# The opening of a two-layer backbone step, gone through input block by input block

## What is computed

```python
D_MODEL, D_FF, SEQ, DEC_SEQ = 1024, 2816, 128, 512
def _mods(cvec, w_ada, b_ada):
    m = jax.nn.silu(cvec) @ w_ada + b_ada
    return m.reshape(cvec.shape[0], 1, N_MOD, D_MODEL)
def _modulate(x, mods, i):
    return x * (1.0 + mods[:, :, 3 * i + 1]) + mods[:, :, 3 * i]
def _swiglu(u, w_up, w_down):
    a, g = jnp.split(u @ w_up, 2, axis=-1)
    return (jax.nn.silu(g) * a) @ w_down
def _ffn_sublayer(x, mods, i, w_up, w_down, ln_g, ln_b):
    y = _swiglu(_modulate(x, mods, i), w_up, w_down)
    return _post_norm(x, y, mods, i, 0.5, ln_g, ln_b)
```

## Time and profile before

| | us |
|---|---|
| median of 3 runs (2974.46 to 2975.7) | 2975.05 |
| the profiled execution, device time | 2975.69 |
| its span, first to last instruction | 2973.9 |
| TensorE matmuls busy in it | 2777.2 (93%) |
| DVE busy | 1711.2 (58%) |
| ACT busy | 766.6 (26%) |

### The profile page before, as it was taken

The page is one execution under the profiler, slowest core; times in us unless marked ns, Lnnn a source line. Parts: engine busy times, 40 slices in busy tenths (PEclk is TensorE's granted clock), DMA queues, the critical chain, the costliest instruction groups (busy, mean ns, idle before and its releaser), DMA issues.

```text
span 2973.9 us, 47454 instructions
## 1 busy us (share of the span) xinstructions
PE 2777.2 (93%) x18760; PEld 2733.3 (92%) x18760; DVE 1711.2 (58%) x3152; ACT 766.6 (26%) x1091; POOL 0.2 (0%) x4
## 2 busy tenths in 40 slices
PE   0599999989999999999999999998999999999994
PEld 0599999989899999999999999998989999999994
DVE  4465555754566685454576555575456668444456
ACT  0211211343322251121252121134332225111124
POOL 0000000000000000000000000000000000000000
PEclk9899999999999999999999999999999999999997
DMA  6233233212133223223313323322213322322320
GB/s 224 79 128 111 102 130 118 79 68 77 54 128 114 99 86 113 99 99 105 117 61 128 113 99 134 114 78 68 77 53 128 114 98 86 113 99 100 112 85 36
DMA packets 76870, 299.34 MB, mean 101 GB/s; under 512 B 24769, under 2 KB 29121, under 8 KB 52673
## 3 DMA queue, kind: packets, MB, share of 16 engines
q1 hardware_dynamic: 50496, 214.31, 20.8%
q10 hardware_dynamic: 26240, 83.20, 8.3%
HBM read 293.80 MB, written 6.82 MB: 101 GB/s over the span
## 4 chain that ended last, share of the span: by engine, by line
PE 89%; DVE 5%; SPq 4%; issue 2%; ACT 1%; DMA 0%; DVEq 0%; ACTq 0%
PE psum L527 11%; PE psum L526 11%; PE psum L524 11%; PE psum L384 6%; PE psum L385 6%; PE psum L382 6%; PE psum L427 3%; PE psum L430 3%; PE psum L431 3%; SPq L299 3%; PE psum L744 3%; PE psum L747 3%; PE psum L746 3%; PE psum L468 2%; PE psum L472 2%
## 5 line engine op out<-in xcount | busy, mean ns | idle before, releaser
L524 PE MATMUL psum<-Uh,w_hi 128*128 128x320 f32 x2304 | 711.9, 309 | 0.0
L526 PE MATMUL psum<-Ul,w_hi 128*128 128x320 f32 x2304 | 711.9, 309 | 0.0
L527 PE MATMUL psum<-Uh,w_lo 128*128 128x320 f32 x2304 | 711.9, 309 | 0.0
L810 ACT ACTIVATE w_hi<-w_raw 128x2048 fp32r<-128x2048 f32 x170 | 325.1, 1912 | 611.4 <-PE psum L382 318.9
L1101 DVE TENSOR_TENSOR w_lo<-w_raw,w_hi 128x2048 fp32r<-128x2048 f32 x170 | 389.5, 2291 | 82.0 <-ACT w_hi L810 76.8
L526 PEld LDWEIGHTS psum<-Ul,w_hi 128*128 128x128 f32 x2304 | 432.5, 188 | 0.0
L527 PEld LDWEIGHTS psum<-Uh,w_lo 128*128 128x128 f32 x2304 | 432.5, 188 | 0.0
L524 PEld LDWEIGHTS psum<-Uh,w_hi 128*128 128x128 f32 x2304 | 432.5, 188 | 0.0
L1284 DVE TENSOR_TENSOR hf<-sg,psum 128x320 f32<-128x320 f32 x176 | 85.7, 487 | 423.6 <-ACT sg L898 421.7
L385 PE MATMUL psum<-Hh,w_lo 128*128 128x320 f32 x1024 | 316.2, 309 | 0.0
L382 PE MATMUL psum<-Hh,w_hi 128*128 128x320 f32 x1024 | 316.2, 309 | 0.0
(11 more groups left out here) (223 smaller groups left out, 5183.7 us busy)
## 6 DMA issues: line engine op xcount, KB each, us to landing
w_raw<-in_wstream SPq DMA_DIRECT2D x188, 1024.0 KB, 4.9
ada_w<-in_ada ACTq DMA_DIRECT2D x145, 512.0 KB, 3.6
ada<-in_ada SPq DMA_DIRECT2D x4, 2048.0 KB, 19.9
gath<-in_rpb SPq DMA_DIRECT2D x128, 24.0 KB, 2.2
G<-gath ACTq DMA_DIRECT2D x4, 768.0 KB, 4.5
X<-in_xT SPq DMA_DIRECT2D x8, 320.0 KB, 14.2
yT<-X SPq DMA_DIRECT2D x8, 320.0 KB, 3.4
mask<-in_mask ACTq DMA_DIRECT2D x2, 384.0 KB, 5.0
```

The source lines that it names most:

```text
L524: m1 = pe.matmul(out, wh, rh, start=(k == 0), stop=False)
L526: pe.matmul(out, wh, rl, start=False, stop=False)
L527: mm = pe.matmul(out, wl, rh, start=False, stop=(k == KD - 1))
L810: act.activation(hi, w_raw[:, r, :, :], ACT.Copy).then_inc(s_whi, 1)
```

## The change

The opening is written as one function on each engine (`opening`), used for the first sub-layer of layer 0; `first_up` stays for the others.
- SyncE loads block by block: two chunks (shift and scale of block k) and x's block k, each a load of its own, into twelve places (`first_w`) used in turn. Blocks 0 and 1 come first, then weight tiles 0 and 1, then blocks 2 to 5, a wait for the first eight sums, blocks 6 and 7, and then the constants. Weight tiles 2 to 19 are loaded by a written-out loop; from tile 4 on, eight gathers follow each load.
- ACT loads `c`, `bada`, `c_ctx`, in this order, with a Silu of one column ahead. It makes u for a block as soon as this block's sums are there, and also the rounded `Uh`, which DVE did before.
- DVE does the sums of blocks 0 and 1 for both vectors; then, for half 0, those of `c` alone for blocks 2 to 7, with the low part `Ul` of the block before in between; and those of `c_ctx` for blocks 2 to 7 in half 1. `bada` (and `bada` + 1, kept in `lnm`) is the sum's starting value. The constants' copies and the scaling of `X` come at the end.
- TensorE goes over the blocks for tiles 0 and 1, from block 4 on with tile 2 too (blocks 0 to 3 of it made up at once), then half 1 of the three, then tile 3 for both halves. At the end it waits for `s_init` 4 and `s_cst`.
- `craw`, `cst` are at other places; the first chunk for the later sums (`load_ada(FIRST_ADA, 0)`) is asked for after tile 3 is rounded.

The declarations are left out here, and the functions `first_up` without `pending`.

```diff
+        def first_mods_ready(v, k):
+
+            if k < 2:
+                return 4 * k + 2 * v + 2
+            return 8 + 2 * (k - 1) + 2 * (KD - 2) * v
...
         @block.sync
         def _(sp):
-            for q in range(4):
-                n = FIRST_ADA // 4
-                sp.dma_start(ada0[:, q * n:(q + 1) * n, :],
-                             a["ada"][q * n:(q + 1) * n].rearrange("c p k -> p c k")).then_inc(s_ada0[q], 16)
-            for k in range(KD):
-                sp.dma_start(X[:, k, :], a["xT"][k]).then_inc(s_x, 16)
-            sp.dma_start(cst[:, :, :], a["dft_small"]).then_inc(s_cst, 16)
+            def first_block(k):
+                for j in range(2):
+                    sp.dma_start(first_w[(2 * k + j) % 12], a["ada"][j * KD + k]).then_inc(s_ada0[k], 16)
+                sp.dma_start(X[:, k, :], a["xT"][k]).then_inc(s_x[k], 16)
+
+            for k in range(2):
+                first_block(k)
+            for s in range(2):
+                sp.dma_start(w_raw[:, s, :, :], a["wstream"][s]).then_inc(s_wload[s], 16)
+            for k in range(2, 6):
+                first_block(k)
+            sp.wait_ge(s_first, first_mods_ready(1, 1))
+            first_block(6)
+            first_block(7)
             sp.dma_start(ident[:, :], a["eye"]).then_inc(s_cst, 16)
             sp.dma_start(lng[:, :], a["lng"]).then_inc(s_cst, 16)
             sp.dma_start(lnb[:, :], a["lnb"]).then_inc(s_cst, 16)
-            for s in range(2):
-                sp.dma_start(w_raw[:, s, :, :], a["wstream"][s]).then_inc(s_wload[s], 16)
-
-            for c in range(QTILE):
-                for r in range(ROWS):
-                    src = a["rpb"][:, ROWS - 1 - r:2 * ROWS - 1 - r, QTILE - 1 - c:QTILE - 1 - c + TW]
-                    sp.dma_start(a["gath"][:, c * ROWS + r, :, :], src).then_inc(s_gath, 16)
-
-            with sp.Fori(1, DEPTH * TILES // 2) as j:
+            sp.dma_start(cst[:, :, :], a["dft_small"]).then_inc(s_cst, 16)
+
+            for t in range(2, 20):
+                sp.wait_ge(s_wsplit, t - 1)
+                sp.dma_start(w_raw[:, t % 2, :, :], a["wstream"][t]).then_inc(s_wload[t % 2], 16)
+                if t >= 4:
+                    c = t - 4
+                    for r in range(ROWS):
+                        src = a["rpb"][:, ROWS - 1 - r:2 * ROWS - 1 - r, QTILE - 1 - c:QTILE - 1 - c + TW]
+                        sp.dma_start(a["gath"][:, c * ROWS + r, :, :], src).then_inc(s_gath, 16)
+
+            with sp.Fori(10, DEPTH * TILES // 2) as j:
...
+            def opening():
+
+
+                def block_products(t, u, h, k):
+                    for b in range(2):
+                        wh, wl = [w[:, b * KD + k, :] for w in t]
+                        rh, rl = half(Uh, Ul, h)(k)
+                        out = bank(u, b, 0, HT)
+                        m1 = pe.matmul(out, wh, rh, start=(k == 0), stop=False)
+                        if (t, h, b, k) == (tiles[0], 0, 0, 0):
+                            started(m1)
+                        pe.matmul(out, wh, rl, start=False, stop=False)
+                        mm = pe.matmul(out, wl, rh, start=False, stop=(k == KD - 1))
+                    if k == KD - 1:
+                        filled(mm)
+
+                tiles = [take(), take()]
+                us = [next_use(), next_use()]
+                for k in range(KD):
+                    if k == 4:
+                        tiles.append(take(spare_f))
+                        us.append(next_use())
+                        for j in range(4):
+                            block_products(tiles[2], us[2], 0, j)
+                    u_ready(0, k)
+                    for t, u in zip(tiles, us):
+                        block_products(t, u, 0, k)
+                us = [next_use() for _ in tiles]
+                for k in range(KD):
+                    u_ready(1, k)
+                    for t, u in zip(tiles, us):
+                        block_products(t, u, 1, k)
+                late = take(spare_h)
+                one(late, 0, 2)
+                one(late, 1, 1)
+                C["u"].next(2 * KD)
+                pe.wait_ge(s_init, 4)
+                pe.wait_ge(s_cst, 64)
...
-            pe.wait_ge(s_init, 3)
-            pe.wait_ge(s_cst, 64)
...
+            def opening():
+
+                def first_input(h, k):
+                    i = h * KD + k
+                    act.wait_ge(s_first, first_mods_ready(h, k))
+                    if h == 0:
+                        act.wait_ge(s_x[k], 16)
+                    if i >= 4:
+                        act.wait_ge(s_u, i - 3)
+                    for lo, hi, v in SEGS[h]:
+                        q = act.activation(u32[:, k % 4, lo - h * HT:hi - h * HT], X[:, k, lo:hi],
+                                           ACT.Identity, bias=mods[0][:, v, k:k + 1],
+                                           scale=mods[0][:, v, KD + k:KD + k + 1])
+                    q.then_inc(s_u32, 1)
+                    act.wait_ge(s_u32, i + 1)
+                    act.activation(Uh[:, k, h * HT:(h + 1) * HT], u32[:, k % 4, :], ACT.Copy).then_inc(s_fu, 1)
+
+                for v in range(2):
+                    act.dma_start(craw[:, v, :], a["c" if v == 0 else "c_ctx"].partition_broadcast(P))\
+                        .then_inc(s_craw[v], 16)
+                    if v == 0:
+                        act.dma_start(bada[:, :], a["bada"]).then_inc(s_bada, 16)
+                act.wait_ge(s_init, 1)
+                act.activation(warm[:, :], epsc[:, :], ACT.Silu)
+                for v in range(2):
+                    act.wait_ge(s_craw[v], 16)
+                    act.activation(csilu[:, v, :], craw[:, v, :], ACT.Silu).then_inc(s_csilu, 1)
+                first_input(0, 0)
+                round_tile()
+                first_input(0, 1)
+                round_tile(1)
+                first_input(0, 2)
+                first_input(0, 3)
+                act.wait_ge(s_csilu, 2)
+                round_tile(2, spare_f)
+                for k in range(4, KD):
+                    first_input(0, k)
+                for k in range(3):
+                    first_input(1, k)
+                gate_half()
+                gate_half()
+                for k in range(3, 6):
+                    first_input(1, k)
+                gate_half()
+                for k in range(6, KD):
+                    first_input(1, k)
+                act.wait_ge(s_first, first_mods_ready(1, KD - 1))
+                round_tile(2, spare_h)
+                load_ada(FIRST_ADA, 0)
+                for _ in range(3):
+                    gate_half()
+                round_tile(1)
+                ada_pair()
+                gate_half()
+                gate_half()
+                ada_pair()
...
+            def opening(chunks):
+
+                taken = [0]
+
+                def first_mod(v, k):
+                    for j in range(2):
+                        if taken[0]:
+                            dve.wait_ge(s_first, taken[0])
+                        start_at = (bada[:, k:k + 1], lnm[:, 0, 0, k:k + 1])[j]
+                        dve.tensor_tensor_reduce(junk[:, :], first_w[(2 * k + j) % 12], csilu[:, v, :], 1.0, start_at,
+                                                 ALU.mult, ALU.add, mods[0][:, v, j * KD + k:j * KD + k + 1])\
+                            .then_inc(s_first, 1)
+                        taken[0] += 1
+
+                def first_low(h, k):
+                    cols = slice(h * HT, (h + 1) * HT)
+                    dve.wait_ge(s_fu, h * KD + k + 1)
+                    dve.tensor_tensor(Ul[:, k, cols], u32[:, k % 4, :], Uh[:, k, cols].bitcast(F32), ALU.subtract)\
+                        .then_inc(s_u, 1)
+
+                dve.wait_ge(s_bada, 16)
+                dve.tensor_scalar(lnm[:, 0, 0, :], bada[:, KD:2 * KD], 1.0, None, ALU.add).then_inc(s_init, 1)
+                dve.wait_ge(s_init, 2)
+                for k in range(2):
+                    dve.wait_ge(s_ada0[k], 32)
+                    for v in range(2):
+                        dve.wait_ge(s_csilu, v + 1)
+                        first_mod(v, k)
+                low_tile()
+                low_tile()
+                for k in range(KD):
+                    if k >= 2:
+                        dve.wait_ge(s_ada0[k], 32)
+                        first_mod(0, k)
+                    if k >= 1:
+                        first_low(0, k - 1)
+                    if k == 4:
+                        low_tile(spare_f)
+                first_low(0, KD - 1)
+                first_low(1, 0)
+                first_low(1, 1)
+                for k in range(2, KD):
+                    first_mod(1, k)
+                    first_low(1, k)
+                    if k == 2:
+                        evacuate(0, 0)
+                        evacuate(1, 0)
+                    if k == 5:
+                        evacuate(2, 0)
+                dve.wait_ge(s_first, taken[0])
+                dve.sem_inc(s_adone, 1)
```

(99 more changed lines are left out.)

52 lines of the change are left out of this document (3 added, 49 removed).

## The result

| | before | after |
|---|---|---|
| median, us | 2975.38 (2974.46 to 2975.76) | 2924.91 (2924.3 to 2927.19) |
| profiled execution, us | 2975.69 | 2927.19 |
| its span | 2973.9 | 2925.2 |
| first matmul at | 87.36 | 25.10 |
| TensorE enters the loop at | 170.5 | 117.93 |

The ratio is 0.9831 (95% interval 0.9816 to 0.9846): 50.5 us less, against 50.6 forecast. Both medians are of four runs, the three of before and one beside the runs of after. The profiled execution of after is the slowest of its four; its terms are read against its own span.

What follows compares the result with a forecast made beforehand. TensorE bounds the kernel (2777.2 of 2973.9 us), with 110.0 us of holes at the start. The opening's end moves from 170.7 to 120.1, so 2975.05 - 50.6 = 2924.4 us; own range 2918 to 2931, wider range 2913 to 2936.5.

Steps and rivals of the forecast that it cites:

- DVE's stop for tile 2: In half 0, DVE and ACT wait for the third weight tile to land: a new stop of 9 to 11 us.
- W: Landing time of the third weight tile, with 512 KB more ahead of it than the second tile had before: 43.3 us.
- half 1, k = 1 low: DVE's low part of block 1 in half 1, after the last input of half 0: done at 60.6 us.
- half 1, k = 7 low: DVE's last low part in half 1, after six blocks of 4.5 us and three `evacuate` of 1.29: 91.5 us.
- stop at the loop's entry: At the opening's end, TensorE waits for `s_init` 4 and the constants' copies: 7.0 + 1.6, so 8.6 us.
- slow restart: After the stop for the constants, TensorE starts at half clock for some 14 matmuls: costs 2.0 us.
- the cover before W: The wait of 9 to 11 us for the third tile hides all that the opening's earlier steps cost.
- lock-step of ACT and DVE in half 1: In half 1, k = 2 to 7, nothing overlaps: 4.5 us a block, DVE idle for 1.4 in each.
- Tile 2 early: Rival: the third tile lands by 33 us, served out of order; chain 10.4 us shorter, 2914; chance 0.10.
- Loads slower: Rival: the opening's small loads go one after the other, 15.6 MB landing at 75 us; 2956; chance 0.05.
- The spread gathers hold the weights back: Rival: gather groups on SyncE take over 14.1 us and delay 16 weight tiles; 2987 at 18 us; chance 0.02.
- The clock takes the slack: Rival: TensorE stays at 1.2 GHz in half 1, which ends at 106.5, 11.1 later; 2935.5; chance 0.10.

Runs made afterwards that it cites:

- extra sums: The changed kernel with four more sums of 128x1024 on DVE before the first low tile: 2927.18 us, again 2926.02.
- early constants: The changed kernel with the constants' copies moved ahead of `evacuate(3, 1)`: 2915.49 us.
- skew: The changed kernel with context's sums of block k + 1 done before the low part of block k in half 1: 2915.55 us.
- sums together: The changed kernel with context's sums of blocks 2 to 7 done right after those of c in half 0 again: 2924.5 us beside 2926.05.

## Why the prediction was right

| step | forecast | measured |
|---|---|---|
| first matmul | 25 to 28 | 25.10 |
| DVE's stop for tile 2 | 9 to 11 | 11.15 |
| tile 2 lands (W) | 43.3 | 42.98 |
| tile 2 low | 47.7 | 47.2 |
| half 1, k = 1 low | 60.6 | 59.9 |
| half 1, k = 7 low | 91.5 | 91.0 |
| tile 3's first matmul | 95.4 | 94.72 |
| the four tiles end | 109.5 | 109.0 |
| stop at the loop's entry | 8.6 | 8.89 |
| loop entered | 118.1 | 117.93 |
| slow restart | 2.0 | 2.9 in this execution |

The steps up to the loop's entry hold to 0.7 us each; 0.3 of the chain's excess stood in W already. DVE's stop is 0.15 us over its range. The restart is off by 0.9. Three were put to the test singly: W by its place in the queue, the cover before W by the extra sums, the stop by the early constants. The lock-step of ACT and DVE in half 1 (1.50 us of DVE idle, forecast 1.4) was tested by the skew.

*Tile 2 early* as a rival fell with W: the landing order is that of the queue. *Loads slower* fell too: with loads of 512 and 320 KB, 406 GB/s were moved at 25 to 30 us, as much as with loads of 2048 KB before (410 at 20 to 25). So the rule of the Trainium skill ("DMA: Bandwidth & Descriptors", section "Measured (HBM→SBUF, 128 partitions, SWDGE, issued from GpSimd)"), to batch to 1 MiB or more, doesn't hold for this full queue of SyncE's; loads issued from GpSimd, of which that section is, no run here has. *The spread gathers hold the weights back* fell in the kernel where they are spread alone: 24 us won, and TensorE's waits after 215 us sum to 62.3 us, as they do in the kernel before; in the changed kernel they are 62.2. *The clock takes the slack* came true in its first half: the clock did fall at the start of half 1 and again before its block 6. I had argued that at half clock TensorE would run without a pause and win the clock back; it did, and half 1 wasn't late for it. It had slack for that, 2.7 us of work at full clock in a block of 4.53. The pauses of up to 2 us in each block, which this rival began from, were not there: TensorE started half 1 behind DVE and ran from 66.45 to 83.96 without a wait, then paused once, for 2.58 us.

Off were only sizes. The slow restart was put at 2.0 and took 2.9 in the profiled execution. The first matmul of the loop starts at 170.50 in the kernel before, and 170.7 is where the matmuls of the last tile end, so the entry moved by 52.6 us, as in the forecast, whose two ends were both 0.2 late. Of these, 2.9 went in the restart and 1.0 later in the program, where TensorE's waits are the same (more half clock there would do it, but no row here shows that); that leaves the 48.7 us of span, less than the 50.6 of the forecast, while the medians, 50.5 apart, meet it. One working was off too: from 126.56 to 130.16 13 matmuls start and not 14, which makes that restart 1.7 us and not 1.5. That the forecast and the medians meet so closely is in part luck, as executions lie up to 3 us apart.

## What to carry to other kernels

Before a queue is reordered, add up the bytes that stand ahead of each operand, and compare the landing with the time when the engines get to it: here one weight tile, late in line, made 11 us of idle time that hid the sums, and moving its load up the queue was worth 7.7 us, nearly as much as a finer order of the arithmetic (9.4). A one-time conversion belongs in an idle moment of its engine before the wait on it, not behind the engine's next long job. And where two engines hand a result back and forth, issue the next input's work ahead of the wait for the last one.

## What was not expected of the hardware

The length of a pause of TensorE didn't settle at which level of the clock it went on. In the kernel with the sums together one pause of 1.97 us, one of 2.03 and one of 2.68 were followed by matmuls at the lower clock, and another of 2.03 and another of 2.68 were not. One of 1.30 us was not (the skewed kernel), nor were ones of 3.27 and 2.90 us in the kernel with tile 2 loaded early, of which this row is the second:

```profile
78.39 0.42 PE L542 MATMUL psum<-Uh,w_hi 128*128 128x320 f32 x1 [2.90 <-DVE Ul L1425]
```

After the pause of 8.9 us at the loop's entry, 13 to 23 matmuls ran slowly, a cost of 1.7 to 2.9 us. It differed between kernels that had the same pause, and between two executions of one kernel (20 and 14 with the extra sums), and I can't say what sets it.
